# Cross-attention scores from high and low parts of queries and keys, with the parts made beside the query projection

## The chip, the cores and the metric

The kernel runs on one core of one Trainium2 chip. The metric is the device time of one execution in microseconds. A core has five engines that run their own instruction streams and meet at semaphores: PE (TensorE, matrix products), DVE (VectorE), ACT (ScalarE), POOL (GpSimd) and SP, which here only issues transfers. PE reads a stationary operand (a weight load, shown as PEld) and streams a moving one. Results land in eight PSUM banks of 128 partitions by 512 fp32 columns.

## What is computed

The program is a decoder trunk of two layers on 512 tokens of 1024 features, with 256 memory tokens. Each layer has a token mixer (three kinds of attention), a cross-attention into the memory, and a SwiGLU network, each between two RMS norms. The part that matters is the cross-attention:

```python
def memory_cross_attention(h, mem_n, w_q, w_kv, w_o):
    B, S, _ = h.shape
    q = (h @ w_q).reshape(B, S, X_HEADS, X_HD)
    kv = (mem_n @ w_kv).reshape(B, mem_n.shape[1], 2, X_HEADS, X_HD)
    k, v = kv[:, :, 0], kv[:, :, 1]
    s = jnp.einsum('bshd,bmhd->bhsm', q, k, preferred_element_type=jnp.float32) * X_HD ** -0.5
    p = jax.nn.softmax(s, axis=-1)
    o = jnp.einsum('bhsm,bmhd->bshd', p.astype(v.dtype), v).reshape(B, S, D_MODEL)
    return o @ w_o
```

There are 4 heads of 256 features; `h` is the normed state and `mem_n` the normed memory. All data are fp32.

## The kernel before

Activations lie feature-major: 8 tiles (`KT`) of 128 features by 512 tokens. Weights come from HBM as 127 units per layer of 128 x 1024 fp32 through a ring of four slots (`RING`): SP loads `raw`, ACT rounds it to `w_hi` (type fp32r, L991, `split_until`), DVE subtracts to get `w_lo` (L1364, `lo_until`), and PE multiplies. ACT may round unit n only when PE has finished unit n - 4. Every projection uses `three` (L554 to L558): three products of rounded parts, w_hi by h_hi, w_hi by h_lo and w_lo by h_hi, all summed in one bank. The activations' parts are `h_hi` (ACT, L1002) and `h_lo` (DVE, L1351).

Nothing is scheduled by a planner: each engine's order is the order of the code. Around the cross-attention, in each layer:

- PE: memory keys (`xk`, 8 tiles with 256 moving columns, from `m_hi` and `m_lo`), memory values (`xv`, 8 units), query projection (`xq`, 8 tiles of 24 products; after tile 0 one fp32 product sums squares for the norm, L603), then the attention, then the output projection `xo`.
- ACT, while PE does keys and values: empties each key tile into `k_x` (L1039), rounds weights, and makes `h_hi` and squares `sq` of the query input, one feature tile at every second step. Then it copies the values, `v_x` (L1288, four copies), rounds weight units 3 and 4 of the query projection (L1290), makes the norm factor `rstd` (L1291), and rounds the units up to the fourth of `xo` (L1292).
- DVE, in the same stretch: residual, `w_lo`, `h_lo` and the sum `acc` of squares. `beside_memory` (L1719) sets its order: for the last feature tile (k = 7), `h_lo` (in `query_input(KT - 1)`, L1727) comes after the low part of unit 3 of the query projection (L1724). The query tiles are then emptied from PSUM, multiplied by `rstd`, into `q_x` (L1734). `xq` uses two banks in turn, so tile 2 on PE waits until tile 0 has been emptied.
- The attention itself works in 16 units (head by block of 128 queries). PE computes the scores of unit u (L906: two plain fp32 products per unit, one for each feature tile of the head; each shows as two records with 128 x 256 outputs), then transposes the probabilities of unit u - 3 (L779, two records), and after each head's last unit multiplies by the values (L916, eight records, `x_out`). DVE masks and takes the row extreme (L1628), inverts the sum (L1636) and scales (L1637). ACT takes the exponential (L1213) and copies the transposes to `pt_x` (L1207). Each head's output is split to `h_hi` (ACT L1297) and `h_lo` (DVE L1739). There are four score banks, so scores of unit u wait for the mask of unit u - 4.

## Time and profile before

| | us |
|---|---|
| median of 3 runs | 1653.84 (1652.95 to 1658.39) |
| the profiled execution's own time | 1652.7 |
| its span, first to last instruction | 1650.9 |
| PE busy | 1580.6 (96%) |
| DVE busy | 896.4 (54%) |
| ACT busy | 721.4 (44%) |
| POOL busy | 20.1 (1%) |
| mean granted TensorE clock | 0.994 of full |

The span is set by PE nearly everywhere; what the other engines do costs time only where PE waits for them. Times in the trace are microseconds from the span's start. Layer 0 has its query projection from 328.7 and its attention from 374.3; layer 1 from 1141.3 and 1186.9. A record of PE is longer than the time until the next one starts, because products are pipelined: the pace is read from start to start.

### The profile page before, as it was taken

How to read it: one execution, taken by the hardware profiler on the slowest of the kernel's cores; microseconds unless marked ns; L12 is line 12 of the kernel's file. 1: busy time of each engine (PE TensorE's matmuls, PEld its weight loads, DVE VectorE, ACT ScalarE, POOL GpSimd, SP SyncE). 2: the span in 40 equal slices, each digit the busy share in tenths (PEclk: the TensorE clock that was granted, in tenths of full speed). 3: DMA queues.
4: the chain of work that ended last, by engine and by line, in shares of the span. 5: the costliest groups of instructions: out<-in, count | busy, mean ns of one | idle time of the engine just before them, and what ended most of it. 6: DMA issues, size and time to landing. Idle time of an engine off the chain costs nothing.

```text
span 1650.9 us, 19229 instructions
## 1 busy us (share of the span) xinstructions
PE 1580.6 (96%) x7420; PEld 1240.5 (75%) x7420; DVE 896.4 (54%) x1388; ACT 721.4 (44%) x1216; POOL 20.1 (1%) x26
## 2 busy tenths in 40 slices
PE   7999899999999999999989989999999999999995
PEld 5776568886778888888767655788866888888884
DVE  5766645935375555532287666458445555555223
ACT  5444645624444444422345356455344444444221
POOL 0000010000000000000000001000000000000000
PEclk9999999999999999999999999999999999999998
DMA  6321003630312333332212200235212233333321
GB/s 233 108 74 37 1 21 133 193 101 14 102 52 93 99 102 102 103 114 90 90 52 89 90 13 1 90 114 179 77 39 77 64 102 97 98 100 113 104 64 51
DMA packets 38538, 143.47 MB, mean 87 GB/s; under 512 B 4272, under 2 KB 4400, under 8 KB 37936
## 3 DMA queue, kind: packets, MB, share of 16 engines
q1 hardware_dynamic: 38448, 142.25, 26.6%
q8 instruction: 59, 0.97, 0.2%
q14 instruction: 31, 0.25, 0.0%
HBM read 140.13 MB, written 2.10 MB: 86 GB/s over the span
## 4 chain that ended last, share of the span: by engine, by line
PE 90%; DVE 5%; ACT 3%; issue 2%; DMA 0%; SPq 0%; DVEq 0%; ACTq 0%
PE bank L556 26%; PE bank L558 25%; PE bank L557 25%; PE bank L808 2%; PE bank L838 2%; PE bank L916 2%; PE bank L906 2%; PE bank L825 1%; PE bank L748 1%; DVE x L1439 1%; PE bank L737 1%; PE bank L603 1%; PE bank L852 1%; DVE acc L1345 1%; DVE y_f L1435 1%
## 5 line engine op out<-in xcount | busy, mean ns | idle before, releaser
L556 PE MATMUL bank<-h_hi,w_hi 128*128 128x512 f32 x1312 | 523.6, 399 | 22.1 <-DVE h_lo L1351 14.7
L1364 DVE TENSOR_TENSOR w_lo<-raw,w_hi 128x1024 fp32r<-128x1024 f32 x254 | 310.7, 1225 | 405.8 <-ACT w_hi L991 403.6
L557 PE MATMUL bank<-h_lo,w_hi 128*128 128x512 f32 x1312 | 513.3, 391 | 0.0
L558 PE MATMUL bank<-h_hi,w_lo 128*128 128x512 f32 x1312 | 513.2, 391 | 0.0
L991 ACT ACTIVATE w_hi<-raw 128x1024 fp32r<-128x1024 f32 x254 | 266.6, 1051 | 256.5 <-PE bank L558 249.8
L556 PEld LDWEIGHTS bank<-h_hi,w_hi 128*128 128x128 f32 x1312 | 247.6, 189 | 89.3 <-issue 24.4
L557 PEld LDWEIGHTS bank<-h_lo,w_hi 128*128 128x128 f32 x1312 | 248.1, 189 | 53.3 <-issue 3.4
L558 PEld LDWEIGHTS bank<-h_hi,w_lo 128*128 128x128 f32 x1312 | 247.9, 189 | 52.6
L556 PE MATMUL bank<-a_hi,w_hi 128*128 128x512 f32 x352 | 136.9, 389 | 0.0
L557 PE MATMUL bank<-a_lo,w_hi 128*128 128x512 f32 x352 | 136.9, 389 | 0.0
L558 PE MATMUL bank<-a_hi,w_lo 128*128 128x512 f32 x352 | 136.9, 389 | 0.0
L1345 DVE TENSOR_TENSOR acc<-acc,sq 128x512 f32<-128x512 f32 x84 | 58.1, 691 | 83.2 <-ACT sq L1010 81.7
L1320 ACT ACTIVATE a_hi<-sq 128x512 fp32r<-128x512 f32 x44 | 27.8, 632 | 140.7 <-DVE sq L1773 140.7
L1010 ACT ACTIVATE sq<-bank 128x512 f32<-128x512 f32 x48 | 28.6, 596 | 127.7 <-PE bank L558 127.7
L557 PEld LDWEIGHTS bank<-a_lo,w_hi 128*128 128x128 f32 x352 | 66.1, 188 | 13.8
L558 PEld LDWEIGHTS bank<-a_hi,w_lo 128*128 128x128 f32 x352 | 66.1, 188 | 13.8
L556 PEld LDWEIGHTS bank<-a_hi,w_hi 128*128 128x128 f32 x352 | 66.1, 188 | 13.5
L1315 ACT ACTIVATE acc<-sq 128x512 f32<-128x512 f32 x44 | 27.8, 632 | 110.0 <-DVE sq L1766 110.0
L1002 ACT ACTIVATE h_hi<-x,gains 128x512 fp32r<-128x512 f32 x48 | 34.6, 722 | 51.7 <-DVE x L1439 50.5
L556 PE MATMUL bank<-m_hi,w_hi 128*128 128x256 f32 x128 | 37.7, 295 | 1.6 <-ACT k_x L1039 1.1
L1687 DVE COPY pt_mix<-bank 128x384 f32<-128x384 f32 (+1 forms) x36 | 21.7, 602 | 30.9 <-PE bank L825 30.1
L1246 ACT ACTIVATE p_mix<-p_mix,stat 128x128 f32<-128x128 f32 (+2 forms) x72 | 35.7, 499 | 3.9 <-DVE stat L1676 3.9
(207 smaller groups left out, 1828.4 us busy)
## 6 DMA issues: line engine op xcount, KB each, us to landing
raw<-w_in SPq DMA_DIRECT2D x254, 512.0 KB, 3.6
x<-x_in SPq DMA_DIRECT2D x4, 512.0 KB, 7.6
mem<-mem_in SPq DMA_DIRECT2D x2, 1024.0 KB, 4.9
out<-x SPq DMA_DIRECT2D x4, 512.0 KB, 2.6
consts<-c_in SPq DMA_DIRECT2D x1, 1600.0 KB, 12.4
mem_sq<-mem_in SPq DMA_DIRECT2D x1, 1024.0 KB, 6.8
gains<-g_in SPq DMA_DIRECT2D x1, 80.0 KB, 3.4
```

What stands on the lines that cost most here:

```text
L556: pe.matmul(out_ap, l_hi, r_hi, start=start, stop=False)
L557: pe.matmul(out_ap, l_hi, r_lo, start=False, stop=False)
L558: return pe.matmul(out_ap, l_lo, r_hi, start=False, stop=stop)
L808: mm = pe.matmul(score_bank(c, i)[:, at:at + n], q[:, qb * P:n], k[:, 0:n], start=(part == 0), stop=(part == last))
L838: mm = pe.matmul(outs[pair % 2][64 * i:64 * i + 64, q0 * P:(q0 + rows.stop - rows.start) * P], mix_head(2 * pair + i)["v"](kb), pt_mix[:, ...
L906: mm = pe.matmul(bank_t[:, 0:N_MEM], q_x[:, 2 * head + c, qb * P:(qb + 1) * P], k_x[:, 2 * head + c, :], start=(c == 0), stop=(c == 1))
L916: mm = pe.matmul(outs[c][:, :], v_x[:, kb, col:col + P], pt_x[:, head % 2, kb, :], start=(kb == 0), stop=(kb == 1))
L991: act.activation(w_hi[:, s, :], raw[:, s, :], ACT.Copy).then_inc(split_hi, 1)
L1002: act.activation(h_hi[:, k, :], x[:, k, :], ACT.Copy, scale=gains[:, layer, g + k:g + k + 1])\
L1246: act.activation(p, p, ACT.Exp, scale=-1.0, bias=stat[:, 0, u:u + 1], accum_out=stat[:, 1, u:u + 1]).then_inc(mix_at["exped"], 1)
L1345: ins = dve.tensor_tensor(acc[:, :], acc[:, :], sq[:, c % 2, :], ALU.add)
L1364: dve.tensor_tensor(w_lo[:, s, :], raw[:, s, :], w_hi[:, s, :].bitcast(F32), ALU.subtract)\
```

## The change

The scores are no longer two fp32 products per unit. They are computed by `three` from rounded parts of queries and keys, three products for each of the two feature tiles, six in all. The parts need room and work:

- `k_hi` and `k_lo` are new names for the buffers `m_hi` and `m_lo`, which are free when the memory projections are done. ACT rounds `k_x` to `k_hi` in four instructions of 128 x 512 (one per head), placed after the value copies and ahead of the two roundings of weights at L1290 of before. DVE subtracts to `k_lo` in four instructions, after the low part of unit 4 of the query projection and ahead of the emptying of the first query tile.
- `q_hi` takes the place of `y_x`, `q_lo` that of `q_x`. ACT rounds each query tile as soon as it is emptied, one instruction of 128 x 512 per tile, each behind the rounding of one more unit of weights. DVE subtracts tile m - 1 after emptying tile m, and tile 7 last.
- At the first unit of each head PE also waits for the low parts of that head.

```diff
+            with ExitStack() as outside:
+                y_x = sb("y_x", [P, KT, SEQ], F32, outside)
+            q_hi = sb("q_hi", [P, KT, SEQ], F32R, room)
...
+            with ExitStack() as whole_q:
+                q_x = sb("q_x", [P, KT, SEQ], F32, whole_q)
+            q_lo = sb("q_lo", [P, KT, SEQ], F32R, room)
...
+        k_hi, k_lo = m_hi, m_lo
...
+                        if qb == 0:
+                            pe.wait_ge(xk_lo, count(xk_lo, layer, head + 1))
+                            pe.wait_ge(xq_lo, count(xq_lo, layer, 2 * head + 2))
                         for c in range(2):
-                            mm = pe.matmul(bank_t[:, 0:N_MEM], q_x[:, 2 * head + c, qb * P:(qb + 1) * P],
-                                           k_x[:, 2 * head + c, :], start=(c == 0), stop=(c == 1))
+                            f, rows = 2 * head + c, slice(qb * P, (qb + 1) * P)
+                            mm = three(bank_t[:, 0:N_MEM], q_hi[:, f, rows], q_lo[:, f, rows], k_hi[:, f, :], k_lo[:, f, :],
+                                       c == 0, c == 1)
...
+                    for head in range(X_HEADS):
+                        act.activation(k_hi[:, 2 * head:2 * head + 2, :], k_x[:, 2 * head:2 * head + 2, :], ACT.Copy)\
+                           .then_inc(xk_hi, 1)
                     split_until(U_XQ + RING + 1)
                     make_rstd("x_pre", D_MODEL)
+                    for m in range(KT):
+                        split_until(U_XQ + m + RING + 1)
+                        wait_emptied(act, layer, use_of("xq", m))
+                        act.activation(q_hi[:, m, :], q_x[:, m, :], ACT.Copy).then_inc(xq_hi, 1)
                     split_until(U_XO + RING)
...
                     lo_until(U_XQ + RING + 1)
+                    for head in range(X_HEADS):
+                        dve.wait_ge(xk_hi, count(xk_hi, layer, head + 1))
+                        done(dve.tensor_tensor(k_lo[:, 2 * head:2 * head + 2, :], k_x[:, 2 * head:2 * head + 2, :],
+                                               k_hi[:, 2 * head:2 * head + 2, :].bitcast(F32), ALU.subtract), xk_lo)
+
+                    def query_lo(m):
+
+                        dve.wait_ge(xq_hi, count(xq_hi, layer, m + 1))
+                        done(dve.tensor_tensor(q_lo[:, m, :], q_x[:, m, :], q_hi[:, m, :].bitcast(F32), ALU.subtract), xq_lo)
+
                     dve.wait_ge(rstd_ready, count(rstd_ready, layer, NORM_AT["x_pre"] + 1))
                     for m in range(KT):
                         lo_until(U_XQ + m + RING)
                         use = use_of("xq", m)
                         wait_tile(dve, layer, use)
                         done(dve.tensor_tensor(q_x[:, m, :], dense[use % 2][:, :], rstd[:, :], ALU.mult), emptied_dve)
+                        if m:
+                            query_lo(m - 1)
+                    query_lo(KT - 1)
```

The instructions in order show where the new ones stand. ACT in layer 0, from the square of the last feature tile to the first exponential; before (`m_hi<-k_x` is the key part, the `w_hi` rows are roundings of weight units):

```order
L1010 ACTIVATE sq<-x 128x512
L1288 ACTIVATE v_x<-bank 128x512 x4
L991 ACTIVATE w_hi<-raw 128x1024 x2
L1026 ACTIVATE rstd<-bank,fixed 128x512
L1028 ACTIVATE rstd<-rstd 128x512
L991 ACTIVATE w_hi<-raw 128x1024 x7
L1213 ACTIVATE p_x,stat<-p_x,stat 128x256 x3
```

and with the change (the pair `q_hi`, `w_hi` comes seven times, of which the first is shown, and an eighth `q_hi` last):

```order
L1020 ACTIVATE sq<-x 128x512
L1298 ACTIVATE v_x<-bank 128x512 x4
L1301 ACTIVATE m_hi<-k_x 128x512 x4
L1001 ACTIVATE w_hi<-raw 128x1024 x2
L1036 ACTIVATE rstd<-bank,fixed 128x512
L1038 ACTIVATE rstd<-rstd 128x512
L1308 ACTIVATE q_hi<-q_x 128x512
L1001 ACTIVATE w_hi<-raw 128x1024
```

Four key roundings now stand between the value copies and the next two weight units, and a query rounding ahead of each later unit.

DVE at the same place, before (`h_lo` with `acc` behind it is the last feature tile of the query input):

```order
L1345 TENSOR_TENSOR acc<-acc,sq 128x512
L1364 TENSOR_TENSOR w_lo<-raw,w_hi 128x1024
L1351 SCALAR_TENSOR_TENSOR h_lo<-x,gains,h_hi 128x512
L1345 TENSOR_TENSOR acc<-acc,sq 128x512
L1364 TENSOR_TENSOR w_lo<-raw,w_hi 128x1024
L1734 TENSOR_TENSOR q_x<-bank,rstd 128x512 x2
```

and with the change:

```order
L1362 TENSOR_TENSOR acc<-acc,sq 128x512
L1381 TENSOR_TENSOR w_lo<-raw,w_hi 128x1024
L1368 SCALAR_TENSOR_TENSOR h_lo<-x,gains,h_hi 128x512
L1362 TENSOR_TENSOR acc<-acc,sq 128x512
L1381 TENSOR_TENSOR w_lo<-raw,w_hi 128x1024
L1748 TENSOR_TENSOR m_lo<-k_x,m_hi 128x512 x4
L1761 TENSOR_TENSOR q_x<-bank,rstd 128x512 x2
L1754 TENSOR_TENSOR q_lo<-q_x,q_hi 128x512
```

The order up to `acc` is the same; four key subtractions stand ahead of the first `q_x`. At the end of the query projection DVE with the change has, ahead of the first mask (`ISA p_x,stat`):

```order
L1761 TENSOR_TENSOR q_x<-bank,rstd 128x512
L1754 TENSOR_TENSOR q_lo<-q_x,q_hi 128x512 x2
L1645 ISA p_x,stat<-bank,consts 128x256
```

where before the first mask followed the last `q_x` at once. On PE one unit's scores and the transposes behind them are

```order
L562 MATMUL bank<-m_hi,q_hi 128x256
L563 MATMUL bank<-m_lo,q_hi 128x256
L564 MATMUL bank<-m_hi,q_lo 128x256
L562 MATMUL bank<-m_hi,q_hi 128x256
L563 MATMUL bank<-m_lo,q_hi 128x256
L564 MATMUL bank<-m_hi,q_lo 128x256
L785 MATMUL bank<-consts,p_x 128x128 x2
```

where before they were `L906 MATMUL bank<-k_x,q_x 128x256 x2` and the same transposes.

## Rows read from the trace of the kernel before

**Rows 1.** Timeline, PE in layer 0's attention: start, duration, engine, line, operation, count.

```profile
374.32 3.72 PE L906 MATMUL bank<-k_x,q_x 128*128 128x256 f32 x16 [0.78 <-DVE q_x L1734]
...
378.10 1.03 PE L906 MATMUL bank<-k_x,q_x 128*128 128x256 f32 x4
378.96 0.38 PE L779 MATMUL bank<-consts,p_x 128*128 128x128 f32 x2
379.18 1.03 PE L906 MATMUL bank<-k_x,q_x 128*128 128x256 f32 x4
...
383.52 3.60 PE L916 MATMUL bank<-pt_x,v_x 128*128 128x512 f32 x8
...
398.86 3.67 PE L916 MATMUL bank<-pt_x,v_x 128*128 128x512 f32 x8 [0.38 <-DVE h_lo L1739]
```

**Rows 2.** Timeline, PE in the memory key projection: rounded products with 256 columns.

```profile
287.01 0.28 PE L556 MATMUL bank<-m_hi,w_hi 128*128 128x256 f32 x1
287.13 0.28 PE L557 MATMUL bank<-m_lo,w_hi 128*128 128x256 f32 x1
```

**Rows 3.** Timeline, DVE at the attention's pace: masks of two units.

```profile
378.57 0.42 DVE L1628 CUSTOM_DVE_ANT_0 p_x<-bank,consts 128x256 f32<-128x256 f32 x1
...
379.62 0.42 DVE L1628 CUSTOM_DVE_ANT_0 p_x<-bank,consts 128x256 f32<-128x256 f32 x1
```

**Rows 4.** Timeline, DVE and ACT where the query projection ends.

```profile
373.57 0.69 DVE L1734 TENSOR_TENSOR q_x<-bank,rstd 128x512 f32<-128x512 f32 x1 [2.99 <-PE bank L558]
373.63 1.06 ACT L991 ACTIVATE w_hi<-raw 128x1024 fp32r<-128x1024 f32 x1 [4.38 <-PE bank L558]
...
375.60 0.42 DVE L1628 CUSTOM_DVE_ANT_0 p_x<-bank,consts 128x256 f32<-128x256 f32 x1 [1.33 <-PE bank L906]
...
377.12 0.35 DVE L1637 TENSOR_SCALAR p_x<-p_x,stat 128x256 f32<-128x256 f32 x1
```

**Rows 5.** Timeline, ACT, then DVE, where the query projection begins.

```profile
328.53 2.04 ACT L1288 ACTIVATE v_x<-bank 128x512 f32<-128x512 f32 x4
330.44 1.07 ACT L991 ACTIVATE w_hi<-raw 128x1024 fp32r<-128x1024 f32 x1
334.62 1.06 ACT L991 ACTIVATE w_hi<-raw 128x1024 fp32r<-128x1024 f32 x1 [3.11 <-PE bank L558]
...
331.61 1.23 DVE L1364 TENSOR_TENSOR w_lo<-raw,w_hi 128x1024 fp32r<-128x1024 f32 x1 [1.56 <-ACT w_hi L991]
332.76 0.74 DVE L1351 SCALAR_TENSOR_TENSOR h_lo<-x,gains,h_hi 128x512 fp32r<-128x512 f32 x1
...
335.78 1.23 DVE L1364 TENSOR_TENSOR w_lo<-raw,w_hi 128x1024 fp32r<-128x1024 f32 x1 [1.55 <-ACT w_hi L991]
```

**Rows 6.** Timeline, PE: last products of query tile 0, in both layers; start of tile 2.

```profile
333.27 0.39 PE L558 MATMUL bank<-h_hi,w_lo 128*128 128x512 f32 x1
333.56 0.50 PE L556 MATMUL bank<-h_hi,w_hi 128*128 128x512 f32 x1
...
340.74 0.39 PE L556 MATMUL bank<-h_hi,w_hi 128*128 128x512 f32 x1
...
1146.16 0.50 PE L556 MATMUL bank<-h_hi,w_hi 128*128 128x512 f32 x1
```

**Rows 7.** Timeline, ACT in the SwiGLU stage: a rounding of 128 x 512 from SBUF.

```profile
599.72 0.63 ACT L1320 ACTIVATE a_hi<-sq 128x512 fp32r<-128x512 f32 x1 [3.35 <-DVE sq L1773]
600.25 1.04 ACT L991 ACTIVATE w_hi<-raw 128x1024 fp32r<-128x1024 f32 x1
```

**Rows 8.** Timeline, PE: idle times of two microseconds elsewhere.

```profile
174.23 1.13 PE L808 MATMUL bank<-k_nope,q_nope 64*128 64x512 f32 x4 [2.05 <-DVE stat L1676]
...
827.26 0.47 PE L556 MATMUL bank<-h_hi,w_hi 128*128 128x512 f32 x1 [2.15 <-issue]
```

**Rows 9.** Stretches: length, busy (count) of PE, PEld, DVE, ACT, POOL; clock; DMA.

```profile
827.30:836.60 9.30, 7.98 (x27) 5.97 (x27) 8.99 (x14) 3.64 (x7) 0.00 (x0) 0.82 0.10 33
...
175.00:200.00 25.00, 23.04 (x184) 14.00 (x181) 16.08 (x51) 14.15 (x45) 1.89 (x2) 1.00 0.01 2
```

More of the change, by code:

```diff
@@ L259 @@
     "ml_inverted": ML_PAIRS, "ml_out": ML_PAIRS, "ml_hi": ML_PAIRS, "ml_lo": ML_PAIRS,
-    "xv_ready": 4, "ff_gate": FT, "ff_exp": FT, "ff_step": 2 * FT, "ff_a": FT, "ff_hi": FT, "ff_lo": FT,
+    "xv_ready": 4, "xk_hi": X_HEADS, "xk_lo": X_HEADS, "xq_hi": KT, "xq_lo": KT, "ff_gate": FT, "ff_exp": FT, "ff_step": 2 * FT, "ff_a": FT, "ff_hi": FT, "ff_lo": FT,
 }
@@ L333, in build @@
             tn_x = sb("tn_x", [P, 2, SEQ], F32, room)
-            y_x = sb("y_x", [P, KT, SEQ], F32, room)
+            with ExitStack() as outside:
+                y_x = sb("y_x", [P, KT, SEQ], F32, outside)
+            q_hi = sb("q_hi", [P, KT, SEQ], F32R, room)
             mem = sb("mem", [P, KT, N_MEM], F32, room)
@@ L337, in build @@
             m_lo = sb("m_lo", [P, KT, N_MEM], F32R, room)
-            q_x = sb("q_x", [P, KT, SEQ], F32, room)
+            with ExitStack() as whole_q:
+                q_x = sb("q_x", [P, KT, SEQ], F32, whole_q)
+            q_lo = sb("q_lo", [P, KT, SEQ], F32R, room)
             k_x = sb("k_x", [P, KT, N_MEM], F32, room)
@@ L391, in build @@
         xv_ready = sem("xv_ready")
+        xk_hi, xk_lo, xq_hi, xq_lo = sem("xk_hi"), sem("xk_lo"), sem("xq_hi"), sem("xq_lo")
         mix_copied = sem("mix_copied_act"), sem("mix_copied_dve")
```

## The prediction

> **What bounds the kernel now.** I read the page first: PE is busy 96% of the span (table above), so an edit is worth what it does to PE's stream, and work of ACT or DVE counts only where PE waits for it. Then the timeline of the stage that the change speeds up, the attention, engine by engine, and then the stage in which it puts the new work, the start and the end of the query projection. In the attention PE goes without idle time: 16 score records in 3.56 us (374.32 to 377.88, that is 378.10 less 0.22), then per unit 0.86 of scores and 0.22 of transposes, 1.08 in all [rows 1]. But DVE needs 1.05 per unit [rows 3], so PE leads it by 0.03 only. At the start of the query projection the reader is to see that PE's last feature step starts at 333.56, not 0.23 after 333.27, and that its record has 0.50: PE has just waited 0.06 for `h_lo` of the last feature tile, which ran from 332.76 to 333.50 [rows 5, 6]. Layer 1 shows the same 0.50 at 1146.16 [rows 6]. That tile has no slack at all.
>
> **The scores.** A unit loses four records of 0.217 (0.86) and gets six rounded products of the same shape as those of the key projection, 128 x 256, which follow each other at 0.12 (287.01, 287.13) [rows 2]: 0.72. So PE saves 0.14 per unit and its pace becomes 0.94. If PE alone set the pace, 16 units would save 2.3 us per layer; that is the upper end. But DVE's 1.05 now stands above PE's 0.94, and DVE starts later (next part). I follow it unit by unit. The first mask moves from 375.60 to 376.0; the first probability, scaled from 377.12 with 0.35, was ready at 377.47 [rows 4], and is at 377.9. PE, ready at 377.2 (374.32 + 16 x 0.18), makes the first transposes at 377.9, the same time as before (377.88). Up to the first product with the values six transposes follow at DVE's 1.05 instead of PE's 1.08: 5 x 0.03 = 0.15, so that product starts at about 383.3 instead of 383.52 [rows 1]. It takes 3.4 us, in which DVE and ACT catch up with the scores already there, so the next four units run nearer to PE's own pace: 4 x 0.14 = 0.56 at most, less a wait of 0.1 to 0.2 for the first head's `h_lo`. This wait exists already at the third product with the values, 0.38 us before 398.86 [rows 1]; it is where DVE stays the bound. The second product gains 0.5 to 0.6, the third 0.8 to 1.2; behind it only transposes remain. I take **1.0 us per layer**, with ends 0.4 (all at DVE's pace: 16 x 0.03) and 2.3.
>
> The trace shows the two fp32 products of a unit as four records of 0.22 and a rounded product as one of 0.12 [rows 1, 2]. The Trainium skill, page "FP8 and Floating Point Precision", section "TensorE Precision Notes", says that true FP32 takes four passes through the array (high by high, the two mixed ones, low by low). By that rule three of four passes would leave 0.65 per unit, and the PE-only saving would be 3.5 us per layer, not 2.3; the measured 0.12 decides, and under DVE's pace neither is reached.
>
> **The end of the query projection.** The four query subtractions and roundings in mid-stage lie under PE's 5.4 us per tile: DVE has idle stretches of 2.99 and ACT of 4.38 there [rows 4], against one instruction of about 0.7 and one of 0.63 more. The last ones don't hide. DVE's last `q_x` ends at 374.26; `q_lo` of tile 6 takes 0.72 to 374.98. `q_hi` of tile 7 stands behind ACT's rounding of a weight unit, 373.63 plus 1.0, plus 0.63: 375.25. `q_lo` of tile 7 then ends at 375.96, and the masks, queued behind it on DVE, start at 376.0, 0.4 late. PE itself waits for tiles 0 and 1 only and starts at 374.32 as before. The 0.4 is in the sum above. PE's new waits at later heads find parts made long before.
>
> **The start of the query projection.** This is the term that decides. The four `k_hi` roundings stand on ACT ahead of the weight unit at 330.44. A rounding of that shape occupies ACT for 0.53 (599.72 to 600.25) [rows 7], four of them 2.12. That unit's rounding moves to 332.56, and DVE's `w_lo` of it, which started at 331.61 when the rounding was done, to 333.73; it has no slack, since DVE had been idle 1.56 for it [rows 5]. `h_lo` of the last feature tile is queued behind it on DVE and moves from 332.76 to 334.88, ending 335.62. PE's step at 333.56 waits for exactly that: **2.12 us per layer**, with nothing under it, as PE's next work is in program order behind. `acc` moves by the same amount and costs nothing further. The bounds: 1.9 if ACT drains the four at 0.48 each, as its value copies do (four in 2.04, the last about 0.6: 1.44 / 3) [rows 5]; 2.5 if each takes its whole 0.63.
>
> Next in DVE's queue are four `k_lo`, about 0.72 each, 2.9 us, ahead of the first `q_x`. `w_lo` moves from 335.78 to 337.90 and ends its share at 339.04; `k_lo` to 341.9; `q_x` of tile 0 to 342.6. PE needs it for tile 2, at 340.74 + 2.12 = 342.86 [rows 6]. Cover is left by 0.2 us, so I cost it at nothing; a slower `k_lo` by 0.1 each would cost 0.2 per layer. Transfers are not moved in a way that counts: a slot's load follows its `w_lo` and has three further tiles of 5.4 us until it is needed.
>
> **The sum.** Per layer +2.1 - 1.0 = +1.1; two layers +2.2 us. On the profiled execution's own time of 1652.7 that is 1654.9. The median of the runs lies 1.1 above that execution, so on the runs' scale I expect 1656.0, that is 0.13% slower, which is inside 0.3% (5 us), about the smallest difference that a measurement of this kernel can tell from none.
>
> **Rivals.**
> *PE alone sets the attention's pace.* DVE would have to overlap masks and scaling more tightly than 1.05. The saving is 2 x 2.3, the sum -0.4: 1653.4. Against it: DVE's pace is steady where PE's was slower.
> *The key roundings are hidden.* If the last `h_lo` had slack, only the attention's -2.0 would remain: 1651.8, and with the full pace 1649.2. Against it stands the 0.50 record in both layers.
> *The clock falls, and the kernel is slower.* The new wait makes an idle time of 2.1 us in PE in each layer. An idle time of 2.15 before 827.26 was followed by a granted clock of 0.82 over the next 9.3 us [rows 8, 9]: that is (0.18 / 0.5) x 9.3 = 3.35 us at 1.2 instead of 2.4 GHz, 1.7 us of work lost. Against it: the idle time of 2.05 before 174.23 left the next 25 us at 1.00 [rows 8, 9]. Before 827 there had been other waits as well, here only dense work. One fall gives 1657.7, two 1659.4, slower beyond 0.3%; it decides from the second fall on.
> *The weight loads come out.* Six products need six stationary loads. Were each product as long as its load record, about 0.19, a unit would have 6 x 0.19 + 0.22 = 1.36, 0.28 above 1.08, or 4.5 us per layer: with the start's 2.1 that is +13, 1669. The 0.12 of the key projection [rows 2], with the same loads, speaks against it. The Trainium skill, page "TensorE: Matmul & The Clock Gate", section "LDWEIGHTS (loading the stationary operand)", gives the load as columns / 1.2 ns, 107 ns here. Unhidden loads by that figure would make 6 x 0.21 of a unit, an estimate of +17 us in all; the trace's key projection disagrees with loads that aren't hidden.
>
> **How the numbers follow.** Forecast 0.50; one or two clock falls 0.22 (two of them 0.06); PE's own pace 0.11; hidden roundings 0.06; weight loads 0.06; a late first `q_x` or other small losses on top 0.05. The range that holds 8 in 10 goes from 1651.8 (hidden roundings) to 1659.5 (two falls); the bounds of the two costs (1.9 to 2.5, 0.4 to 2.3) lie within: 1653.0 to 1658.1. Slower by over 0.3% (above 1658.8): two falls, weight loads and part of the rest, 0.14. Faster by over 0.3% (below 1648.9): 0.02. Within: 0.84.
>
> **What would show it.** In the new profile PE should wait about 2.1 us for the last `h_lo` (L1368) at about 333.5 and again in layer 1, with four ACT roundings `m_hi<-k_x` just ahead. The six products of a unit should start 0.12 apart; the first mask should start about 2.4 us after the last `q_x` starts, instead of 2.03; PE should show small idle times ahead of transposes (L785) in the first head. Query tile 2 should start without a wait. PEclk should read full in both query projections. I am wrong if PE doesn't wait for `h_lo`, if the products are spaced wider between transposes than in the key projection, or if the attention gains nothing or over 2 us per layer.

## The result, and the profile after

The changed kernel takes 1658.54 us (median of 17 runs, 1657.73 to 1662.37), the kernel before 1653.81 (17 runs, 1651.97 to 1658.88). The ratio is 1.0032, with a 95% interval of 1.0025 to 1.0038: 4.7 us slower by the medians. One of 29 executions of the kernel before on another chip took 2296 us at a clock of 0.655 and is left out of every comparison. The forecast of 1656.0 had the sign and was 2.5 us too low. The result lies in the range because the range reached to the rival of the falling clock. Of the line at 0.3% the medians stand just inside (0.29%) and the ratio just outside.

The profiled execution of the changed kernel was its slowest, 1662.37 us, 9.7 above the profiled one of before. So a difference of the two profiles as wholes misleads, and I compare them from milestone to milestone: the first product of each norm sum and the first product of each group of products with the values. The shift of the second profile against the first grows at these places:

| stretch | layer 0 | layer 1 |
|---|---|---|
| program start to the first norm sum | +2.07 | |
| start of the query projection | +2.10 | +2.09 |
| first value product | -0.14 | -0.13 |
| second value product | -0.38 | -0.38 |
| third value product | -0.11 | -0.11 |
| three stretches at a lower clock that before didn't have | +1.32 (at 462) | +1.62 (at 998), +1.6 (at 1155) |

The first line is not the change's: the first norm sum starts between 32.0 and 34.6 us in the profiles of all kernels here, at 32.5 and at 33.7 in two executions of the same kernel before; the changed kernel's three profiles have it 2.07, 1.79 and 0.12 later than the first profile of before. The waits that the change makes and removes come to +1.5 per layer, +2.9 in all. The clock's stretches come to +4.5 in this execution. The medians of the runs differ by 4.7, which leaves 1.8 for the clock and for whatever else there is.

The page of after: busy time of each engine. PE's holds the stretches at half clock too.

```profile
PE 1582.5 (95%) x7484; PEld 1242.5 (75%) x7484; DVE 913.2 (55%) x1412; ACT 733.4 (44%) x1240; POOL 20.1 (1%) x26
```

The start of the query projection in layer 0, timeline of ACT, then of DVE, then of PE (start, duration, engine, line, operation, count, idle time before and what ended it); it answers to [rows 5, 6]. All starts contain the 2.07 of the program's start.

```profile
330.63 2.04 ACT L1298 ACTIVATE v_x<-bank 128x512 f32<-128x512 f32 x4
332.53 2.21 ACT L1301 ACTIVATE m_hi<-k_x 128x512 fp32r<-128x512 f32 x4
334.62 1.07 ACT L1001 ACTIVATE w_hi<-raw 128x1024 fp32r<-128x1024 f32 x1
...
335.79 1.22 DVE L1381 TENSOR_TENSOR w_lo<-raw,w_hi 128x1024 fp32r<-128x1024 f32 x1 [3.64 <-ACT w_hi L1001]
336.94 0.74 DVE L1368 SCALAR_TENSOR_TENSOR h_lo<-x,gains,h_hi 128x512 fp32r<-128x512 f32 x1
...
341.11 2.86 DVE L1748 TENSOR_TENSOR m_lo<-k_x,m_hi 128x512 fp32r<-128x512 f32 x4
344.01 0.69 DVE L1761 TENSOR_TENSOR q_x<-bank,rstd 128x512 f32<-128x512 f32 x1
...
335.36 0.39 PE L564 MATMUL bank<-h_hi,w_lo 128*128 128x512 f32 x1
337.73 0.50 PE L562 MATMUL bank<-h_hi,w_hi 128*128 128x512 f32 x1 [1.98 <-DVE h_lo L1368]
...
344.91 0.40 PE L562 MATMUL bank<-h_hi,w_hi 128*128 128x512 f32 x1
```

Read it from below. PE is idle 1.98 and is released by `h_lo`. `h_lo` stands on DVE behind `w_lo`, DVE was idle 3.64 for ACT's `w_hi` (before: 1.56), and in front of that `w_hi` on ACT stand the four roundings, from 332.53 to 334.62: 2.09. The same lines show that the four `k_lo` cost PE nothing: `q_x` of tile 0 ends at 344.70, and PE starts tile 2 at 344.91.

The attention in layer 0, timeline of DVE, then of PE; it answers to [rows 1, 3, 4].

```profile
377.77 0.69 DVE L1761 TENSOR_TENSOR q_x<-bank,rstd 128x512 f32<-128x512 f32 x1 [2.76 <-PE bank L564]
...
379.51 0.69 DVE L1754 TENSOR_TENSOR q_lo<-q_x,q_hi 128x512 fp32r<-128x512 f32 x1 [0.32 <-ACT q_hi L1308]
380.24 0.42 DVE L1645 CUSTOM_DVE_ANT_0 p_x<-bank,consts 128x256 f32<-128x256 f32 x1
...
378.52 0.39 PE L562 MATMUL bank<-m_hi,q_hi 128*128 128x256 f32 x1 [0.79 <-DVE q_x L1761]
378.74 0.28 PE L563 MATMUL bank<-m_lo,q_hi 128*128 128x256 f32 x1
378.86 0.28 PE L564 MATMUL bank<-m_hi,q_lo 128*128 128x256 f32 x1
...
382.02 0.44 PE L785 MATMUL bank<-consts,p_x 128*128 128x128 f32 x2 [0.36 <-DVE p_x L1654]
...
387.57 3.60 PE L926 MATMUL bank<-pt_x,v_x 128*128 128x512 f32 x8
394.96 3.67 PE L926 MATMUL bank<-pt_x,v_x 128*128 128x512 f32 x8
...
402.43 3.67 PE L926 MATMUL bank<-pt_x,v_x 128*128 128x512 f32 x8 [0.38 <-DVE h_lo L1769]
```

The rounded products follow each other at 0.12 (378.74, 378.86), loads of new stationary tiles included. The first mask starts 2.47 after the last `q_x`, before it was 2.03. PE now waits for DVE ahead of transposes (0.36), where it had not waited before, and ahead of the third value product it still waits the same 0.38 as before [rows 1]. From the scores' start to that product the stage gained 0.63.

The clock. A stretch of after, then the same of before, at the start of the query projection in layer 1, where the last column but two is the granted clock (the columns are those of [rows 9]):

```profile
1152.00:1162.00 10.00, 8.03 (x26) 5.42 (x25) 7.17 (x9) 3.30 (x5) 0.00 (x0) 0.83 0.34 105
```

```profile
1152.00:1162.00 10.00, 10.00 (x46) 8.29 (x45) 3.83 (x4) 2.12 (x2) 0.00 (x0) 1.00 0.21 72
```

A mean of 0.83 over 10 us is 3.4 us at 1.2 GHz. If dense matmul work lost half of it, that would be 1.7; the milestones show 1.6. Before, the stretch is at 2.4 GHz throughout. It comes right behind the new idle time. But in layer 0 of the same execution the same idle time is followed by no fall, and there are two new falls at 462 and 998, far from any edit. Below, a "fall" is such a stretch of about 3.4 us. One costs 1.3 to 1.6 at some places and nothing at others.

The places far from the edit have idle times of their own. PE in the changed kernel, just ahead of those two falls:

```profile
461.90 0.47 PE L562 MATMUL bank<-h_hi,w_hi 128*128 128x512 f32 x1 [2.15 <-DVE h_lo L1368]
...
998.52 0.81 PE L831 MATMUL bank<-consts,p_mix 128*128 128x128 f32 x3 [1.96 <-DVE pt_mix L1704]
```

and in the kernel before at the first of them, which has no fall there in this execution:

```profile
458.29 0.47 PE L556 MATMUL bank<-h_hi,w_hi 128*128 128x512 f32 x1 [2.15 <-DVE h_lo L1351]
```

This holds for all twelve profiles of this text: past the first 25 us and ahead of the last 20, they have 28 falls, and each begins right behind an idle time of PE of 1.9 to 2.2 us, with its end or up to 1.5 us after it. In that part the kernel before has seven such idle times, ending near 174, 181, 458, 827, 987, 994 and 1271; the change adds two. Which of them are followed by a fall differs between executions.

### The profile page after: what moved, and what is told of

Its sections match the earlier page's. It is cut to its first block, busy times and chain, and to the rows that moved or that the text cites. A ratio compares the mean times of both kernels' runs of the same rounds, so it can differ in the third digit from the quotient of the medians.

```text
span 1660.5 us, 19435 instructions
## 1 busy us (share of the span) xinstructions
PE 1582.5 (95%) x7484; PEld 1242.5 (75%) x7484; DVE 913.2 (55%) x1412; ACT 733.4 (44%) x1240; POOL 20.1 (1%) x26
## 4 chain that ended last, share of the span: by engine, by line
PE 85%; DVE 8%; ACT 3%; issue 3%; DMA 0%; SPq 0%; DVEq 0%; ACTq 0%
PE bank L562 25%; PE bank L563 24%; PE bank L564 24%; PE bank L814 2%; PE bank L926 2%; PE bank L844 2%; PE bank L831 1%; DVE x L1456 1%; DVE w_lo L1381 1%; DVE h_lo L1368 1%; PE bank L754 1%; DVE acc L1362 1%; PE bank L609 1%; PE bank L743 1%; DVE y_x L1452 1%
## 5 line engine op out<-in xcount | busy, mean ns | idle before, releaser
L1012 ACT ACTIVATE h_hi<-x,gains 128x512 fp32r<-128x512 f32 x48 | 34.6, 722 | 53.1 <-DVE x L1456 50.5
L1368 DVE SCALAR_TENSOR_TENSOR h_lo<-x,gains,h_hi 128x512 fp32r<-128x512 f32 x48 | 36.0, 749 | 2.6 <-ACT h_hi L1012 1.6
```

The costliest lines, as they stand in the source:

```text
L1012: act.activation(h_hi[:, k, :], x[:, k, :], ACT.Copy, scale=gains[:, layer, g + k:g + k + 1])\
L1368: done(dve.scalar_tensor_tensor(out=h_lo[:, k, :], in0=x[:, k, :], scalar=gains[:, layer, g + k:g + k + 1], in1=h_hi[:, k, :].bitcast(F32) ...
```

## The experiments

The questions. How large are the two effects of the waits, each by itself? Where do the remaining 1.8 us of the medians come from: the new idle time (through the clock), the mere shift of all later work, or another wait? And what bounds the gain in the attention?

**Noise of the milestones.** The kernel before once more, without an edit.

> The kernel before once more, unchanged, for a second profile. It shows what differs between two executions of the same program: when the first products start (8.1 us in the first profile of before, 9.6 in that of the changed kernel, whose whole start lies 2.07 us later), and how often the granted clock falls to half for 3.4 us (after the idle times at 827 and 1271 in the first profile). If the start differs by executions, it lies anywhere between 8 and 10 us here; the query projection of layer 1 should show full clock.

It took 1653.88. The program's start was 1.14 later than in the first profile; the four steps at the query projection and the attention were +0.03, -0.01, 0 and 0. So a milestone step is good to some 0.05 (the largest step in untouched work of any kernel here, outside the falls, is 0.10), while the start of the program is good to 2 us. Even between these two executions one costly fall had moved: one at 462 (+1.32) in place of one at 1272 (-1.34).

**The changed kernel again**, twice.

> The changed kernel once more. Waits alone: in each layer PE waits 2.1 us for the last h_lo and gains 0.6 us in the attention, 2 x 1.5 = +3.0 us, ratio 1.0018. Waits and clock: the new idle time is followed by a fall of the clock in some executions, 1.6 us each, so the ratio is 1.0025 to 1.0038 as measured, and the profile shows a granted clock under 1 in a query projection of one layer or both. If the 1.8 us beyond +3.0 came by a later start or by chance, the clock is full there.

> The changed kernel a third time, beside e9_delay_only on the same chip: ratio 1.0033, mean clock 0.993. Waits repeat to 0.05 us (start of the query projection +2.1, attention -0.63 per layer); the falls need not. If the new idle times cause them, about half of the query projections show one (3 of 6 in the profiles of the changed kernel and of e5_parts_fp32 so far).

The first took 1658.41 beside 1653.66, ratio 1.0033 (1.0020 to 1.0045), the second 1657.85 beside 1653.39, ratio 1.0029 (1.0017 to 1.0040). The steps by waits were those of the first profile to within 0.05: +2.1, about -0.14, -0.38, -0.11 in each layer. The clock was not. The first had no fall in either query projection, with the same 2 us of idle time in PE; its stretch in layer 1:

```profile
1152.00:1162.00 10.00, 9.16 (x38) 7.10 (x39) 7.74 (x12) 4.37 (x6) 0.00 (x0) 1.00 0.32 105
```

The second had one in both, layer 0 first:

```profile
330.00:340.00 10.00, 8.02 (x27) 5.50 (x26) 4.75 (x7) 6.07 (x10) 0.00 (x0) 0.84 0.33 107
...
1152.00:1162.00 10.00, 10.00 (x36) 7.52 (x35) 6.12 (x10) 4.53 (x6) 0.00 (x0) 0.83 0.29 99
```

So the +2.9 repeats in every execution, and the falls vary from one to the next.

**The key roundings behind the weight unit.** One line is put ahead of the `k_hi` loop on ACT, so that the weight unit that PE needs is rounded first.

```diff
+                    split_until(U_XQ + RING)
                     for head in range(X_HEADS):
                         act.activation(k_hi[:, 2 * head:2 * head + 2, :], ...
```

> The changed kernel with the four key roundings behind the next weight unit instead of ahead of it (still ahead of the one after). Waits alone: the wait for h_lo falls from 2.1 us to the old 0.06 in both layers, 4.2 us less than the changed kernel, about 0.5 us above before (ratio 1.0003). Waits and clock: with the idle time the falls behind it go too, so up to 1.8 us less than that, 1.3 us below before (0.9992). If the key roundings are not what delays h_lo, the time stays that of the changed kernel (1.003).

It took 1651.50 beside 1653.66, ratio 0.9994 (0.9985 to 1.0002). ACT, then DVE, in layer 0:

```profile
330.64 1.08 ACT L1001 ACTIVATE w_hi<-raw 128x1024 fp32r<-128x1024 f32 x1
331.59 2.21 ACT L1302 ACTIVATE m_hi<-k_x 128x512 fp32r<-128x512 f32 x4
...
331.82 1.22 DVE L1382 TENSOR_TENSOR w_lo<-raw,w_hi 128x1024 fp32r<-128x1024 f32 x1 [1.58 <-ACT w_hi L1001]
332.96 0.74 DVE L1369 SCALAR_TENSOR_TENSOR h_lo<-x,gains,h_hi 128x512 fp32r<-128x512 f32 x1
```

The step at the query projection's start falls from +2.10 to +0.04 (layer 1: +0.03), and the attention keeps its -0.64 and -0.58. The whole is -1.1 by waits. The place of four instructions in ACT's queue is therefore worth 2.1 us per layer; that is shown. With the idle time the falls in the query projections are gone too.

**Half of them.** Two `k_hi` roundings ahead of the unit, two behind it.

```diff
+                    for head in range(2):
+                        act.activation(k_hi[:, 2 * head:2 * head + 2, :], ...
+                    split_until(U_XQ + RING)
+                    for head in range(2, X_HEADS):
```

> The changed kernel with two of the four key roundings ahead of the weight unit and two behind it. Each rounding ahead delays h_lo by its 0.53 us on ACT, so the wait is 1.05 to 1.1 us instead of 2.1 and the profile lies between the changed kernel and e3_key_late: +0.9 us over before by waits alone (1.0005). If the falls of the clock need the longer idle time, they go as in e3_key_late (mean clock 0.9945); if they come after the short one too, the mean clock is 0.993 and the ratio 1.0015.

It took 1654.66, ratio 1.0007 (0.9999 to 1.0016). PE's wait in layer 0:

```profile
335.90 0.50 PE L562 MATMUL bank<-h_hi,w_hi 128*128 128x512 f32 x1 [0.94 <-DVE h_lo L1372]
```

The step is +1.03 and +1.04, half of 2.10: 0.52 per rounding, with no slack from the first one on. Neither query projection had a fall.

**Cheaper scores without the parts' making.** From the kernel before: `q_x` and `k_x` are rounded as they are written and stand for both parts; the low parts are left out.

```diff
-            q_x = sb("q_x", [P, KT, SEQ], F32, room)
-            k_x = sb("k_x", [P, KT, N_MEM], F32, room)
+            q_x = sb("q_x", [P, KT, SEQ], F32R, room)
+            k_x = sb("k_x", [P, KT, N_MEM], F32R, room)
...
+                            mm = three(bank_t[:, 0:N_MEM], q_x[:, f, rows], q_x[:, f, rows], k_x[:, f, :], k_x[:, f, :],
+                                       c == 0, c == 1)
```

> The kernel before with six rounded products per unit, but no parts made: ACT and DVE write the rounded values directly to k_x and q_x, and the products take them for both parts (the low parts are left out of the computation). PE's pace only: 0.14 x 16 x 2 = 4.6 us less than before (0.9972). DVE's pace of 1.05 as the bound, with the first mask at 375.3 instead of 375.6: 1.6 us per layer less, 3.2 in all (0.9981). If rounded products between transposes cost more than the 0.12 of the key projection, less than that or slower.

It took 1651.35 beside 1653.66, ratio 0.9982 (0.9973 to 0.9991). The steps are +0.03, -0.75, -0.38, -0.11. DVE's first mask and PE's value products in layer 0:

```profile
376.88 0.42 DVE L1629 CUSTOM_DVE_ANT_0 p_x<-bank,consts 128x256 f32<-128x256 f32 x1 [1.18 <-PE bank L558]
...
384.22 3.60 PE L917 MATMUL bank<-pt_x,v_x 128*128 128x512 f32 x8
391.61 3.67 PE L917 MATMUL bank<-pt_x,v_x 128*128 128x512 f32 x8
399.07 2.38 PE L917 MATMUL bank<-pt_x,v_x 128*128 128x512 f32 x5 [0.38 <-DVE h_lo L1740]
```

The mask waits for the first score (PE) here, not for the last part. That is what three rounded products give when nothing is added to the other engines: 1.24 per layer of the 2.3 by which PE's own work shrinks. The expectation had 1.6, by DVE's pace alone; its 3.2 us for both layers stand against 2.4 by the steps, so that the ratio came out as expected (0.9981) is in part luck. PE still waits 0.38 for `h_lo`; what that wait hangs on is read in the part on the attention below. And the changed kernel's 0.63 lacks 0.6 of it at the first value product alone, where its mask stands behind the last parts.

**The parts' making without cheaper scores.** From the changed kernel: the parts are made, but the scores are fp32 products of the high parts read as fp32; the low parts aren't used.

```diff
-                            mm = three(bank_t[:, 0:N_MEM], q_hi[:, f, rows], q_lo[:, f, rows], k_hi[:, f, :], k_lo[:, f, :],
-                                       c == 0, c == 1)
+                            mm = pe.matmul(bank_t[:, 0:N_MEM], q_hi[:, f, rows].bitcast(F32), k_hi[:, f, :].bitcast(F32),
+                                           start=(c == 0), stop=(c == 1))
```

> The changed kernel with all the parts made where they are and all its waits, but the old two fp32 products per unit, of the high parts (the low parts are left out of the scores). The cost of making the parts without the gain: 2.1 us of wait per layer and nothing regained, in the attention 0 to 0.2 us lost by the late first mask, so +4.4 us by waits and about 6 with the falls of the clock, ratio 1.0035 to 1.004. Against the changed kernel it is 1.3 to 1.6 us slower. If the attention's gain in the changed kernel came from something else than the products (1.0033 again), they don't matter.

It took 1661.0 beside 1653.48, ratio 1.0039 (1.0025 to 1.0054). The value products in layer 0:

```profile
386.68 3.60 PE L926 MATMUL bank<-pt_x,v_x 128*128 128x512 f32 x8
394.45 3.60 PE L926 MATMUL bank<-pt_x,v_x 128*128 128x512 f32 x8
402.03 2.38 PE L926 MATMUL bank<-pt_x,v_x 128*128 128x512 f32 x5 [0.38 <-DVE h_lo L1769]
```

They are 7.77 and 7.58 apart, 15.35 together; before, first to third were 15.34 apart (383.52, 398.86) [rows 1], and in the changed kernel 14.86. So the -0.38 and -0.11 belong to the cheaper products alone. The first value product is late by nothing against the scores' start (0.00 in both layers): with the slow scores the late mask is free. The start costs 2.06, as with the cheap ones. This profile has falls right behind the idle time in both layers, the first of which adds 1.62:

```profile
330.00:340.00 10.00, 8.02 (x26) 5.41 (x25) 5.19 (x7) 5.43 (x9) 0.00 (x0) 0.83 0.35 103
...
1152.00:1162.00 10.00, 8.03 (x27) 5.37 (x26) 7.18 (x9) 3.33 (x5) 0.00 (x0) 0.83 0.35 105
```

**The same delay with the idle time filled.** From the changed kernel: two rounds of idle-filling matmuls on constants ahead of PE's wait for the last `h_lo`. They end about when `h_lo` does.

```diff
+                        def before_step(k):
+                            if k == KT - 1:
+                                keep_busy(2)
+                            after_norm("x_pre")(k)
+                        project("xq", m, tiles(h_hi), tiles(h_lo), before=before_step if m == 0 else None)
```

> The changed kernel with two products more on PE, of ones by a constant into a free bank, just ahead of the feature step that waits for the last h_lo: 1.7 us of work in the 2.1 us of idle time, results unused. Path alone: PE's step still starts with h_lo, so the time stays (ratio 1.0033). Clock: without the idle time the falls behind it go; the mean granted clock rises from 0.993 to 0.994 or 0.995 and about 1.8 us come back (1.0021). If the two products end after h_lo, the step is late by what they reach beyond it, under 0.3 us.

It took 1658.41 beside 1653.48, ratio 1.0026 (1.0018 to 1.0035). PE in layer 0, and the two stretches:

```profile
335.05 0.40 PE L564 MATMUL bank<-h_hi,w_lo 128*128 128x512 f32 x1
335.29 1.88 PE L624 MATMUL bank<-consts 128*128 128x512 f32 x4
337.42 0.50 PE L562 MATMUL bank<-h_hi,w_hi 128*128 128x512 f32 x1 [0.25 <-DVE h_lo L1372]
```

```profile
330.00:340.00 10.00, 9.75 (x38) 6.65 (x37) 4.75 (x7) 6.90 (x12) 0.00 (x0) 1.00 0.44 150
...
1152.00:1162.00 10.00, 9.75 (x38) 6.61 (x37) 7.29 (x10) 3.24 (x6) 0.00 (x0) 1.00 0.33 105
```

The waits are the same (+2.08, -0.13, -0.37, -0.12), PE is idle 0.25 instead of 1.98, and the clock stays full in both query projections. Yet the time is that of the changed kernel: by the means of its runs +4.2 against before, 1.3 more than its +2.9 of waits (the interval of the ratio is 3.0 to 5.8 us, with 2.9 at its lower end). Its profile has falls at 462 (+1.32) and 998 (+1.61) instead, behind the old idle times there. The expectation came true for the clock: its mean over the 12 runs is 0.9941, where the changed kernel's three groups of runs have 0.9929 to 0.9932. It did not for the time: of the 1.8 us that were to come back, between 0 and 1 did, as medians, means or ratios are compared.

**The shift alone.** The kernel before, with the same matmuls put behind the wait, so that all later work comes later and nothing else is changed.

```diff
+                        def before_step(k):
+                            after_norm("x_pre")(k)
+                            if k == KT - 1:
+                                keep_busy(2)
+                        project("xq", m, tiles(h_hi), tiles(h_lo), before=before_step if m == 0 else None)
```

> The kernel before with the two products of e8_busy_wait behind the wait for the last h_lo instead of ahead of it: 1.72 us of PE work more per layer and no idle time, the same delay of all that follows as the changed kernel has within 0.3 us. By path +3.4 us, 1.0021, with the mean clock of before (0.9941 to 0.9945). If the falls of the clock come from the later work being shifted, as the costly falls at 998 in three late kernels suggest, and not from the new idle time, the mean clock is 0.993 and about 1.5 us more are lost, 1.0030.

It took 1658.21 beside 1653.39, ratio 1.0030 (1.0018 to 1.0041). By the path it is +1.71 and +1.72 at the two query projections and -0.06 at each first value product, +3.3 in all. Measured are +4.3 (means) and +4.8 (medians), 1.0 to 1.5 more, though the interval of the ratio (3.0 to 6.8 us) still holds 3.3. The expectation had tied the slower time to a mean clock of 0.993 and the faster to that of before. Neither pair came: the clock is 0.9943 over the runs (before, beside it, 0.9946), and the time is the slower one. The falls at 462 (+1.34) and 998 (+1.62) are in the profile. The stretch at 998, of this kernel, then of the changed kernel's second execution, which had no fall there:

```profile
994.00:1003.00 9.00, 7.04 (x44) 4.21 (x42) 5.64 (x21) 5.80 (x20) 0.00 (x0) 0.81 0.00 0
```

```profile
994.00:1003.00 9.00, 7.04 (x48) 3.99 (x46) 6.51 (x21) 7.00 (x23) 0.00 (x0) 1.00 0.00 1
```

PE is busy 7.04 of 9 us in both, and has the same idle time of 1.96 us in both (to 998.34 and to 998.17). So the same idle time is followed by a fall in one execution and not in another, and falls come at the old idle times also where no idle time was added. That the delay costs more than itself is likely by the centre of the interval and not shown.

**The version that the findings point to.** The weight unit first, as above; the `k_lo` subtractions one per query tile, and each last query part as late as its user allows, so that the first masks no longer stand behind them.

```diff
+                            if u == 2 * TB + 1:
+                                ahead()
...
-                    for head in range(X_HEADS):
+                    def key_lo(head):
...
+                        if m:
+                            query_lo(m - 1)
+                        if 2 <= m < 2 + X_HEADS:
+                            key_lo(m - 2)
```

> As e3_key_late, and the rest of the part making put into idle stretches as well: on DVE each query tile's low part ahead of the wait for the next tile, key low parts one per tile from tile 2 on, and the last query low part during the first product with the values. The first mask follows the last q_x as before. By DVE's pace as the bound each layer then gains what e4_no_parts does, 0.75 + 0.38 + 0.11 = 1.24 us, 2.5 in all: ratio 0.9985, one us less than e3_key_late, whose first mask is late. If the late first mask costs nothing, it equals e3_key_late (0.9993).

It took 1652.07 beside 1653.48, ratio 0.9986 (0.9976 to 0.9997). DVE's last `q_x` and first mask, and PE's value products:

```profile
375.19 0.69 DVE L1768 TENSOR_TENSOR q_x<-bank,rstd 128x512 f32<-128x512 f32 x1 [2.46 <-PE bank L564]
377.07 0.42 DVE L1648 CUSTOM_DVE_ANT_0 p_x<-bank,consts 128x256 f32<-128x256 f32 x1 [1.18 <-PE bank L564]
...
384.41 3.60 PE L926 MATMUL bank<-pt_x,v_x 128*128 128x512 f32 x8
391.80 3.67 PE L926 MATMUL bank<-pt_x,v_x 128*128 128x512 f32 x8
399.27 1.96 PE L926 MATMUL bank<-pt_x,v_x 128*128 128x512 f32 x4 [0.38 <-DVE h_lo L1773]
```

The mask starts 1.88 after `q_x` and waits for the scores again. The steps are +0.01, -0.66, -0.38, -0.10: -1.14 per layer, nearly the 1.24 of the version that makes no parts. It computes all that the changed kernel does and is the only full version here whose interval lies wholly below 1, by 0.14% at its centre. That it beats the version with the unit first, as its steps say by 1.1 us, isn't shown by the times: the intervals overlap, and the other's median is the lower one (1651.50).

## Why the prediction was right or wrong

Times in us, this kernel less the one before beside it. "By the ratio" is the measured ratio and its interval, times the median of before.

| kernel | by waits, both layers | medians | by the ratio | mean clock, this and before | falls at the start of the query projections |
|---|---|---|---|---|---|
| changed, first | +2.9 | +4.7 | +5.3 (4.1 to 6.3) | 0.9929, not recorded | 1 of 2 |
| changed, second | +2.9 | +4.75 | +5.5 (3.3 to 7.4) | 0.9932, 0.9941 | none |
| changed, third | +2.9 | +4.5 | +4.8 (2.8 to 6.6) | 0.9931, 0.9946 | 2 of 2 |
| parts, fp32 scores | +4.1 | +7.5 | +6.4 (4.1 to 8.9) | 0.9923, 0.9945 | 2 of 2 |
| idle time filled | +2.9 | +4.9 | +4.3 (3.0 to 5.8) | 0.9941, 0.9945 | none |
| shift alone | +3.3 | +4.8 | +5.0 (3.0 to 6.8) | 0.9943, 0.9946 | none |
| two roundings ahead | +0.8 | +1.2 | +1.2 (-0.2 to 2.6) | 0.9939, 0.9945 | none |
| unit first | -1.1 | -2.2 | -1.0 (-2.5 to 0.3) | 0.9945, 0.9941 | none |
| unit first, parts spread | -2.3 | -1.4 | -2.3 (-4.0 to -0.5) | 0.9939, 0.9945 | none |
| no parts | -2.4 | -2.3 | -3.0 (-4.5 to -1.5) | 0.9946, 0.9941 | none |

**What bounds the kernel** was read rightly: each step in PE's stream came out one for one, and the tile without slack was the place.

**The start of the query projection**: right. 2.12 was predicted, 2.10 and 2.09 measured. The row behind it, 0.53 from one rounding's start to the next instruction [rows 7], was the right price, not its duration of 0.63. Taking it away and halving it confirm the cause.

**The `k_lo` cover** of 0.2 held: 0.21 (344.70, 344.91), and the step costs nothing.

**The attention**: the mechanism was right and the size was not: -0.63 per layer where the sum had -1.0. The first value product came as predicted (-0.2 said, -0.14), with the mask 0.44 late; the second gave -0.52 in total where 0.5 to 0.6 was said. The mis-sized term is the third, 0.8 to 1.2 said and 0.63 measured. The step that failed was to let PE run at nearly its own pace for four more units. The wait of 0.38 for `h_lo` had been read from [rows 1] and named as the place where DVE is the bound; it should have been carried through: where the same producer ends the wait before and after, the later product can gain only what that producer gains. It stayed at exactly 0.38 in every kernel here.

What that producer gains stands one step further back. Layer 0 before, the second value product on PE, then DVE:

```profile
391.29 3.60 PE L916 MATMUL bank<-pt_x,v_x 128*128 128x512 f32 x8
...
395.88 0.42 DVE L1628 CUSTOM_DVE_ANT_0 p_x<-bank,consts 128x256 f32<-128x256 f32 x1 [2.11 <-PE bank L906]
...
398.02 1.42 DVE L1739 TENSOR_TENSOR h_lo<-bank,h_hi 128x512 fp32r<-128x512 f32 x2
```

and DVE with the change:

```profile
399.48 0.42 DVE L1645 CUSTOM_DVE_ANT_0 p_x<-bank,consts 128x256 f32<-128x256 f32 x1 [1.83 <-PE bank L564]
...
401.59 1.42 DVE L1769 TENSOR_TENSOR h_lo<-bank,h_hi 128x512 fp32r<-128x512 f32 x2
```

Behind each value product DVE itself has run out of scores: it is idle 2.11 (1.83) until PE's next ones, masks two units, and makes `h_lo`, which the third value product waits for. From the second value product to that mask it is 4.59 before and 4.52 after, from the mask to `h_lo` 2.14 and 2.11, and from there to the third value product 0.84 in both. So between those products not four units of PE's scores are on the path but one, and what is gained is 0.1 where the sum had 0.3 to 0.6. No run here makes DVE's part shorter by itself, so this is read from the trace and not tried.

I had also priced the late mask into the first product and then given it up as small; by the versions without it, it costs 0.5 to 0.6 of the 1.14 to 1.24 that are to be had, though only with the cheap scores.

**The rivals.** PE's own pace fell: no kernel gained 2.3, the best 1.24. Hidden key roundings fell. The weight loads fell: products with new stationary tiles follow at 0.12, also between transposes. (The 1669 of that rival is a slip: its +13 on before's 1653.8 makes 1667.) The sum of the waits should have been +1.5 per layer, 1655.6 on the profile's scale and 1656.7 on the runs', not 1656.0.

**The clock** is most of what lies between 1656.7 and 1658.54, as far as is known, and the rival was drawn too narrowly. It said that falls would come right behind the new idle times, 1.7 each, and the main text expected none ("PEclk should read full in both query projections"). Such falls do come: in the profiles of kernels with the idle time of 2 us, 5 of the 8 places have one, in all others none, and filling the idle time removes them. The size was right too (1.6). The reason given against the rival, that there is only dense work around the new idle times, did not hold; and the fall behind 827 that it was drawn from costs nothing itself, since the next milestone comes at the same distance in profiles without it (28.2 from 820 to 848).

What the prediction lacked is that the kernel before has seven idle times of the same length, and that a fall comes behind five of them in some executions and not in others; it took before's profile for a fixed base. Counted over the profiles, six of kernels whose work comes 1.7 us or more later from the query projection on, and six of the others:

| idle time that ends near (in before) | cost of a fall there | six delayed | six others |
|---|---|---|---|
| new, 335 and 1153 | 1.6 | 5 of 8 | |
| 174, 181 | none seen | 0 of 12 | 0 of 12 |
| 458 | 1.3 | 5 of 6 | 1 of 6 |
| 827 | 0 | 1 of 6 | 3 of 6 |
| 987 | 0 | 0 of 6 | 2 of 6 |
| 994 | 1.6 | 4 of 6 | 0 of 6 |
| 1271 | 1.3 | 3 of 6 | 4 of 6 |

The delayed kernels have more falls at 458 and 994, where they cost, and fewer at the two places where they don't. This is how a kernel without new idle times can have before's mean clock and still lose time by falls: the profiles of the filled and the shifted kernel have two falls each, as both of before have, but two that cost instead of one. The mean clock of the runs points the same way. One fall lowers it by 0.001. The changed kernel has 0.0010 and 0.0015 less than before, about one fall more per execution; the filled and the shifted one have 0.0004 and 0.0003 less. The kernels with little or no new idle time scatter by up to 0.0006 either way, so the difference between one fall and none is clear of the noise only just.

**What stays open.** How the 1.8 us (1.9 to 2.6 by the ratios) divide between falls behind the new idle times and falls moved to dearer places isn't settled. The excesses of the filled version (1.3 to 2.0) and of the shift alone (1.0 to 1.7) are about as large as half the width of their intervals (1.4 and 1.9), the start of the program adds 2 us of spread to every single run, and six profiles a side suggest the moved falls but don't prove them. No run here fills the old idle times too, which would try it. Nor do the runs show why the same idle time is followed by a fall in one execution and not in the next. The medians of 6 to 12 runs are uncertain by about 1 us themselves: the two versions with the unit first are -2.2 and -1.4 by medians and -1.0 and -2.3 by the ratio, where the waits say -1.1 and -2.3.

## What to carry to other kernels

Before work is put into an engine's queue, find which instruction behind it feeds a tile with no slack: four roundings of 0.52 us each cost 2.1 us on PE, one for one, and the same four behind one weight unit cost nothing. A cheaper product gains only up to the next engine that is already waited for, and a wait for the same producer in the same length before and after says that the gain stops there. Where a change is worth less than the clock moves, list each profile's falls first, with the idle time ahead of each and what it costs there; then compare milestones of the traces step by step, and the whole by many runs. A mean clock counts falls that cost nothing too.

## What the runs showed of the hardware

- The granted clock falls to 1.2 GHz for about 3.4 us at places that differ between executions of the same kernel. All 28 such falls of the twelve profiles begin behind an idle time of PE of 1.9 to 2.2 us. A fall costs 1.3 to 1.6 us where PE is dense, nothing behind 827 and 987, where the next norm sum comes at the same distance with and without one. Five of the eight new idle times had one, none of the four shortened to 0.94 or 0.25 us had, and neither of the two places near 174 and 181 had one in twelve profiles. The stretch from 994 to 1003 had PE busy 7.04 us, and the same idle time of 1.96 us, both with a fall and without one.
- Rounded products of 128 x 256 follow each other at 0.12 us with a new stationary tile for each. The Trainium skill, page "TensorE: Matmul & The Clock Gate", section "LDWEIGHTS (loading the stationary operand)", has a load of 128 columns at 107 ns; it was hidden in full here.
- The same program reaches its first norm sum between 32.0 and 34.6 us. Two profiles can differ by 2 us before any edit is reached.
